# Router and final norm by columns, and the recurrence products between the first projections, in a four-layer fp32 kernel

## What is computed

```python
def rmsnorm(x, g):
    y = xf * lax.rsqrt(jnp.mean(xf * xf, axis=-1, keepdims=True) + EPS)
    return (y * g.astype(jnp.float32)).astype(x.dtype)

# first mixer, HGRN2 part (chunks of 64 tokens, 4 heads of 128)
    scores = jnp.einsum('bhnck,bhnsk->bhncs', q_dec, kh * jnp.exp(-bcum))   # then the causal mask
    o_intra = jnp.einsum('bhncs,bhnsv->bhncv', scores, vh)
    chunk_upd = jnp.einsum('bhnck,bhncv->bhnkv', kh * jnp.exp(b_last - bcum), vh)
    _, S_prev = lax.scan(step, S0, ...)                                     # S = dec * S + upd
    o = o_intra + jnp.einsum('bhnck,bhnkv->bhncv', q_dec, S_prev)           # then a norm per head
```

## Time and profile before

| | us |
|---|---|
| median of three timed runs (2555.94 to 2558.72) | 2557.13 |
| the profiled execution's own time | 2546.73 |
| its span, from the first to the last instruction | 2545.0 |
| the 24 tiles of `even_in` on PE | 25.6 to 110.5 |
| the rest of the first mixer, up to the last tile of `mixT` | 110.5 to 158.9 |
| first tile of `even_out` taken by ACT | 163.5 |
| last S5 output products | 1403.4 to 1409.6 |
| `s5_glu` | 1409.6 to 1466.2 |
| router, up to the first expert product | 1466.2 to 1500.7 |
| experts, up to the last `down` product | 1500.7 to 2519.1 |
| last spread, final norm, output | 2519.1 to 2545.0 |

### The profile page before, as it was taken

One profiled execution on the slowest core, in us unless ns is written; L12 is line 12 of the kernel. 1 busy time (PEld: TensorE's weight loads), 2 busy tenths in 40 slices (PEclk: granted clock), 3 DMA queues, 4 the chain that ended last, 5 costly groups with the idle time before them and its releaser, 6 DMA issues.

```text
span 2545.0 us, 62471 instructions
## 1 busy us (share of the span) xinstructions
PE 2320.7 (91%) x28556; PEld 2047.2 (80%) x28556; DVE 657.6 (26%) x1469; ACT 475.4 (19%) x1019; POOL 75.0 (3%) x31
## 2 busy tenths in 40 slices
PE   7989999998999899999765979999999999999997
PEld 6767887757888767888532778899999889999997
DVE  1334323133322343112699120111110111111102
ACT  2312122122221243001322111111111111111111
POOL 0000000000000000000253000000000000000000
PEclk9979999999999999999877989999999999999999
DMA  7312344232243142344200068989998989998993
GB/s 287 116 54 96 149 155 159 83 116 100 100 155 159 54 166 100 122 159 165 99 0 33 1 277 330 349 339 360 348 360 337 349 328 357 344 355 329 374 347 118
DMA packets 42271, 523.46 MB, mean 206 GB/s; under 512 B 4785, under 2 KB 4914, under 8 KB 5810
## 3 DMA queue, kind: packets, MB, share of 16 engines
q1 hardware_dynamic: 42034, 519.74, 53.0%
HBM read 518.68 MB, written 1.05 MB: 204 GB/s over the span
## 4 chain that ended last, share of the span: by engine, by line
PE 85%; DVE 9%; issue 3%; ACT 2%; DMA 0%; SPq 0%; DVEq 0%; ACTq 0%
PE ps L1244 24%; PE ps L820 17%; PE ps L799 12%; PE ps L1257 12%; PE ps L831 9%; PE ps L781 2%; PE ps L1002 1%; PE ps L1232 1%; DVE scr L1705 1%; PE ps L845 1%; PE ps L1203 1%; DVE rstd L1359 1%; DVE proj L1705 1%; PE ps L945 1%; PE ps L988 1%
## 5 line engine op out<-in xcount | busy, mean ns | idle before, releaser
L1244 PE MATMUL ps<-scr,slot 128*64 128x96 f32 x14336 | 651.5, 246 | 30.2 <-issue 29.2
L1244 PEld LDWEIGHTS ps<-scr,slot 128*64 128x64 f32 x14336 | 619.5, 137 | 37.8 <-issue 37.5
L820 PE MATMUL ps<-hT,slot 128*128 128x256 f32 x2016 | 445.4, 379 | 0.0
L820 PEld LDWEIGHTS ps<-hT,slot 128*128 128x128 f32 x2016 | 383.0, 190 | 52.1
L1257 PE MATMUL ps<-scr,slot 128*64 128x96 f32 x7168 | 354.9, 247 | 19.2 <-issue 19.1
L1257 PEld LDWEIGHTS ps<-scr,slot 128*64 128x64 f32 x7168 | 321.6, 137 | 36.6 <-issue 36.5
L799 PE MATMUL ps<-hT,slot 128*128 128x256 f32 x1120 | 246.5, 381 | 9.7 <-DVE hT L1346 7.6
L799 PEld LDWEIGHTS ps<-hT,slot 128*128 128x128 f32 x1120 | 211.2, 190 | 44.9 <-issue 16.9
L831 PE MATMUL ps<-scr,slot 128*128 128x256 f32 x1056 | 242.3, 383 | 4.8 <-DVE scr L1562 4.8
L831 PEld LDWEIGHTS ps<-scr,slot 128*128 128x128 f32 x1056 | 202.7, 192 | 34.6 <-DVE scr L1562 6.5
L1805 DVE TENSOR_TENSOR scr<-scr,ps 128x96 f32<-128x96 f32 x224 | 56.4, 252 | 649.0 <-PE ps L1244 649.0
(11 more groups left out here) (308 smaller groups left out, 1521.3 us busy)
## 6 DMA issues: line engine op xcount, KB each, us to landing
slot<-in_w_moe SPq DMA_DIRECT2D x224, 1536.0 KB, 8.7
slot<-in_w_ffn SPq DMA_DIRECT2D x33, 3072.0 KB, 10.2
slot<-in_w_even_in SPq DMA_DIRECT2D x4, 3072.0 KB, 22.9
slot<-in_w_odd_qk SPq DMA_DIRECT2D x2, 3072.0 KB, 9.9
slot<-in_w_s_glu SPq DMA_DIRECT2D x2, 3072.0 KB, 10.6
slot<-in_w_odd_v SPq DMA_DIRECT2D x2, 2048.0 KB, 7.9
slot<-in_w_even_out SPq DMA_DIRECT2D x1, 3072.0 KB, 9.9
slot<-in_w_odd_out SPq DMA_DIRECT2D x1, 3072.0 KB, 10.2
```

Of the source, the lines that this page charges most:

```text
L820: m = pe.matmul(pair(f, k), w[:, o:o + P], hT[:, c], start=c == 0, stop=c == KD - 1, skip_group_check=True)
L1244: m = pe.matmul(pair(f, k)[s:s + STRIP, 0:CAP], w[:, o:o + STRIP], xg[e % 2][:, c], start=c == 0, stop=c == KD - 1, skip_group_check=True)
```

## The change

**First mixer.** The weight columns are laid out in another order (0 to 3 forget, 4 to 7 values, 8 to 11 RG-LRU branch, 12 to 15 q, 16 to 19 output gates, 20 to 23 RG-LRU gate), the ring of the projection shrinks to two PSUM banks, and PE puts each group of recurrence products between two projection tiles. ACT and DVE are ordered to match. The last multiplication of the RG-LRU, one of 1024 columns, becomes four of 256 at the end of DVE's chain. No product is added or taken away here.

**S5.** The 16 output products of a group are ordered so that neighbours go to different column groups.

**Router.** DVE multiplies `xT` by the norm weights as each tile is made, inside the loop over `s5_glu`. PE then makes, for each of the 8 tiles, logits from these, the sum of squares with the squares as the stationary side and one column of ones, and the transposes. The root of the mean square is a number per token (per partition) now, and is applied where it matters: to the difference of the two logits and, as a factor, in `pick`. The branch on PE tests for 0 and has the gathered form first, the dense one behind it.

**End.** The last expert spreads over three PSUM banks, and releases `xT` tile by tile. The final norm goes by columns as the router does, the root is applied in the copies, and these are shared by ACT and DVE.

```diff
             def hgrn_rglru():                                  # PE
-                pe.wait_ge(tile_taken, 12)
...
+                for i in range(tiles):
+                    project(i)
+                    if i == 8:
+                        turn_values()
+                    if i == 9:
+                        turn_keys()
+                    if i == 11:
+                        updates()
+                        gate_products(0)
+                        gate_products(1)
+                    if i == 12:
+                        gate_products(2)
+                        gate_products(3)
+                    if i == 16:
+                        scores()
+                    if i in (18, 19):
+                        outputs(i - 18)
+                    if i in (20, 21):
+                        head_sums(i - 20)
...
             def outputs(q):                                    # PE, S5
-                    for j in range(4):
-                        k = 32 * j
-                        terms = [(r, x[q % 2]) for r, x in ((0, sA), (0, sC), (1, sB), (1, sD))]
-                        for i, (r, x) in enumerate(terms):
+                    terms = [(r, x[q % 2]) for r, x in ((0, sA), (0, sC), (1, sB), (1, sD))]
+                    for i, (r, x) in enumerate(terms):
+                        for j in range(4):
+                            k = 32 * j
...
             def router():                                      # PE
-                total("m3")
...
+                for c in range(KD):
+                    pe.wait_ge(h_ready, H0["m3"] + c + 1)
+                    for g in range(2):
+                        pe.matmul(ps[:, 2, g * 8:g * 8 + 8], yT[:, c, g * P:(g + 1) * P],
+                                  wr[:, c, :], start=c == g == 0, stop=c == KD - 1,
+                                  skip_group_check=True)
+                    pe.wait_ge(sq_ready, SQ0["m3"] + c + 1)
+                    for g in range(2):
+                        m = pe.matmul(ps[:, 2, 16 + g:17 + g], sq[:, c, g * P:(g + 1) * P],
+                                      ones[:, 0:1], start=False, stop=c == KD - 1,
+                                      skip_group_check=True)
...
+                        m = pe.transpose(turned_chunk(g, c), yT[:, c, g * P:(g + 1) * P], ident)
...
-                with pe.If(pe.value_load(crowded[0:1, 0:1], min_val=0, max_val=1) == 1):
+                with pe.If(pe.value_load(crowded[0:1, 0:1], min_val=0, max_val=1) == 0):
+                    experts_gathered()
+                with pe.Else():
                     experts_dense()
-                with pe.Else():
-                    experts_gathered()
...
+            def final_norm():                                  # ACT
+                act.activation(stat[:, 0, 0:1], ones[:, 0:1], ACT.Sqrt)
+                for c in range(KD):
+                    act.wait_ge(x_ready, (X_VERSION["mf"] - 1) * KD + c + 1)
+                    act.activation(sq[:, c], xT[:, c], ACT.Square).then_inc(sq_ready, 1)
+                    act.activation(hT[:, c], xT[:, c], ACT.Copy, scale=v("final_norm", c)
+                                   ).then_inc(h_ready, 1)
...
             def router():                                      # DVE
-                pre_norm("m3", xT, hT, "ffn_norm", 8)
...
+                    dve.tensor_scalar(pick[:, g], count, posm[:, g, e:e + 1], col[:, 2 + g:3 + g],
+                                      ALU.is_equal, ALU.mult).then_inc(mo["pick"], 1)
```

More of the change, by code:

```diff
@@ L273, in build_program @@
         rt = {n: sem("rt_" + n) for n in (
-            "logits", "diff", "exp", "comb", "spread", "taken")}
+            "logits", "sums", "root", "diff", "exp", "comb", "spread", "taken", "diag", "hturned")}
+        fin = {n: sem("fin_" + n) for n in ("sums", "root", "rstd")}
+        out_taken_act, out_taken_dve = sem("out_taken_act"), sem("out_taken_dve")
         moe_loaded = [sem(f"moe_loaded{i}") for i in range(HALVES)]
@@ L482, in hgrn_rglru @@
                                ).then_inc(hg["logf"], 1)
-                for i in range(16, 20):
-                    take("even_in", i, xbp[:, i - 16, 3:3 + T])
+                take("even_in", 5, proj[:, 9])
+                take("even_in", 6, proj[:, 10])
                 act.wait_ge(hg["bcum"], 4)
@@ L718, in router @@
             def router():
-                pre_norm("m3")
+                squares("m3", xT, x_ready, (X_VERSION["m3"] - 1) * KD)
+                for n in range(4):
+                    act.wait_ge(mo["hturned"], n // 2 + 1)
+                    g, half = n % 2, n // 2
+                    act.activation(vtok[:, g, half * 512:half * 512 + 512], ps[:, g, :], ACT.Copy
+                                   ).then_inc(mo["htaken"], 1)
+                act.wait_ge(rt["sums"], 1)
+                act.activation(col[:, 0:2], col[:, 24:26], ACT.Sqrt, bias=EPS, scale=1.0 / D
+                               ).then_inc(rt["root"], 1)
                 act.wait_ge(rt["diff"], 2)
```

458 lines of the change are left out of this document (276 added, 182 removed).

## The result

The changed kernel takes **2527.22 us** (median of 4 runs, 2522.43 to 2531.44), the kernel before in the same session 2556.53 (4 runs, 2549.56 to 2558.72): ratio **0.9875, 95% interval 0.9851 to 0.9899**, 1.2% faster. The forecast was 2521.5 with a range of 2505 to 2536. The execution profiled took 2525.31 us, its span is 2523.6 and its mean granted clock 0.964.

A forecast was written before the change was run, and what follows sets the result against it. PE was taken as the bound, with gains only where it idles or runs at half clock: first mixer 23.5, S5 2.0, router 8.1, end 2.0, together 35.6 us; 2557.1 - 35.6 = 2521.5, range 2505 to 2536.

The forecast's parts named there:

- the sum: Whole kernel: gains of 23.5 (first mixer), 2.0 (S5), 8.1 (router) and 2.0 (end) make 35.6 us.
- First mixer, 23.5 forecast: First mixer: products move between projection tiles, first `even_out` tile ends at 140.0 instead of 163.5; gain between 11 and 28.
- five more products end its first tile: Start of `even_out`: three products done when DVE's heads end at 137.8, five more end the first tile at 140.0.
- the second step that failed: First mixer: 56 output records, 0.31 us each at half clock, take half of that at full clock, 8.7 us.
- Rival (b): First mixer: outputs of 64 columns let the clock fall inside the projections; gain 11 to 15, time 2532; chance 0.16.
- S5, 2.0 forecast: Last group of S5 outputs: 32 records take 4.3 us instead of 6.25 by overlapping; gain between 0 and 3.
- Router, 8.1 forecast: Router to experts: PE falls through into the gathered form, first expert product at 1492.5 instead of 1500.65; gain 4 to 12.
- End, gain of 2.0 forecast: End: far branch taken at 3 us, two norm tiles at full clock, six at half; from gain 8 to loss 4.5.
- Rival (c): End and router: no stall at the end and full clock in both column-wise norms; time 2512; chance 0.08.
- (a): End: the far branch costs as much as at the router, losing 4.5 instead of gaining 2; time 2528; chance 0.18.
- (d): Experts: new code position brings 100 more late code fetches, 79 us; time 2600, slower by 43; chance 0.03.
- (e): First mixer: the change fails, for instance ACT's order holds up the ring of two; no gain, 2545; chance 0.05.

The follow-up runs named there:

- the later session: The kernel before and the changed kernel, unaltered, timed again beside a version with four further edits: medians 2556.88 and 2525.5 us, ratio 0.9897.
- the root and the pieces: Changed kernel plus four edits: early root of two heads, mixer outputs in eight pieces, woven router tiles, final norm in both branch arms; 2513.5 us, ratio 0.9846.
- the pieces: Changed kernel with the first mixer's outputs in eight pieces between products of tiles 19 and 20, not two blocks; 2526.41 us, one run, mixer 118.43.
- the arm: Changed kernel with PE's final norm written into both arms of its branch; 2515.9 us, ratio to before 0.9854, end 19.70 us.

## Why the prediction was right or wrong

**The time.** 2527.2 lies in the range and 5.7 above the forecast. On medians the change is worth 29 us (31 in the later session), and that is what the 35.6 of the sum is to be compared with. On the two profiled executions it is 21.4, and taken from them the forecast would have been 2511.1, 14 too low. The difference lies in the profile of before: at 2546.73 it is below all timed runs of its session and within 0.5 us of the fastest of the 11 later ones, 10.4 below the median, while after's is only 1.9 below its own. The sum had no term for that (4.2 us of it stand in the experts and 0.4 in the start, and after's end was 2.4 slower than that of six executions on average), and adding the 10.4 back put it right. Term by term the sum was too large by 7.75 us at the mixer and, against the average of six ends, 0.7 at the end, and too small by 1.35 up to the last S5 output: 7.1, where the medians show 35.6 - 29.3 = 6.3.

**First mixer, 23.5 forecast, 15.75 measured.** The mechanism was right: no recurrence product behind the last projection, PE waiting in `even_out` for `mixT`, DVE's chain last. The size was off by 7.75, and the profile splits it. Up to ACT's taking of tile 21 the stream was 5.9 us longer than worked out (104.97 from its start instead of 99.1): 3.0 in the first unit at half clock, 1.4 because an output takes 0.18 us and not the 0.155 I took as half of the earlier trace rows, 0.3 for the updates (2.91 instead of 2.6), 1.2 for tile 20, which took 4.74 behind the outputs. ACT's and DVE's parts (2.4 and 10.7 us) came out within 0.2 us. The last 1.9 is `even_out` at PEclk 0.64 behind PE's pause; the step "five more products end its first tile" priced them at full clock. So 6.1 of the 7.8 us are the clock (3.0, 1.2 and 1.9), and the step that failed by size is the sum's assumption of PEclk 1.00 from the first record to the last. In other executions the three parts are shared out differently, but the total is the same within 1.6. Where the clock did stay up, the forecast holds: with the root and the pieces the whole stretch ran at 1.00 and took 113.49, against 137.9 - 23.5 = 114.4 (columns as above).

```profile
25.19:138.68 113.49, 112.19 (x565) 94.63 (x566) 46.81 (x76) 43.93 (x68) 1.80 (x1) 1.00 0.31 123
```

That isn't the forecast's kernel, since the root stands ahead of tile 21 in it; that more than makes up for outputs priced too low. This pricing, of an output at half its half-clock time, is the second step that failed, by 1.4 us. I had excluded a fixed time near 0.31 by the scores of the earlier trace rows, 0.064 us a record; but they have weights of 64 columns, the outputs of 128, and full clock took the outputs only to 0.18. Whether the width of the weights makes the difference no run tried. Rival (b) named the fall of the clock, with a gain of 11 to 15, and the pieces confirm it. In size, too, after lies nearer to it than to the forecast.

**S5, 2.0 forecast, 2.8 measured** on the last group. The upper bound of 3 was nearly reached: four records overlap, where the earlier trace rows showed three. The old order gives it back.

**Router, 8.1 forecast, 8.0 measured.** Term by term as well: tiles at 1.1 and 2.2 were 1.07 and 2.02, four and four, the fall came 4.5 us behind the last dense record (4.4 assumed), the first expert product followed 5.64 us behind the pick's start (5.5). The fetch was a conclusion from one row and is now shown: cutting the code that is jumped over removed 6.2 us in the kernel before, and the packet of instructions lies in the stall. Of the gain of 8.0 the inversion made 5.9; with the dense form first again the rest of the router's change gave 2.2 up to the pick (26.78 against 28.99). By the Trainium skill, "Runtime: NRT & Kernel Launch", section "Instruction fetch mechanics", a branch breaks the sequential prefetch; the runs agree, with 5.9 us at the router and 2.65 to 3.13 us of idle time at the end.

**End, gain of 2.0 forecast, loss of 1.1 measured.** The fetch was taken at 3 us between bounds of 1.5 and 8; PE was idle for 3.13. What was off stands around it: in this execution the first spreads ran at a reduced clock (0.9 us each instead of 0.47), and the clock was at 0.50 from the first sum, not after two tiles. In five more executions of the same end the first sum came 9.5 to 9.9 us behind the last `down` instead of 11.67, and the end took 22.8 to 25.2, a gain of 0.7 to 3.1 on before's 25.93. The forecast is right for those. But it did not see the size of the opportunity: the inversion did not pay (5.9 for 7.0 on average), and the rivals that I gave compared ends with a fetch, never the same change without the inversion. Rival (c) asked for no stall and full clock in both norms; the arm gave that at the end alone, and 2515.9 where (c) said 2512.

**Other rivals.** (a) is false: idle for 3.1, not 6 us. That the median, 2527.2, lies next to its 2528 is chance: the 6 us are missing at the mixer instead. (d), more gaps in the experts: 4.2 us more in one pair of executions, 43 were asked for. (e) is false: no wait of L936 for ACT is in the profile.

## What to carry to other kernels

A branch of PE that jumps over long code cost 6 us here beside a full weight stream and 3 us with the DMA idle, and in the second place the work behind it ran at a low clock as well: invert it only if what follows the branch goes into the arm, and look at both ends before counting the gain. Short TensorE records (64 columns, 8, 1) were worth putting between 256-column records, a few at a time: in two blocks of 5 us they slowed themselves and the dense tile behind them. A pause of PE that a data chain forces can cost more than its length, by the clock behind it, so shortening the chain by 3.4 us gave 5.6. And before a sum is made against one profiled execution, look where that execution lies among the timed runs: a sum of stretches is to be taken off the median.

## What the hardware showed that I had not expected

- PEclk fell during busy stretches: PE had no idle time in 119 to 125 (3.00 of 3.00 us), made records of 64 columns up to 121.9 and of 256 behind them, and the clock was 0.81 and then 0.62.
- Records of 64 columns with weights of 128 columns take 0.18 us at full clock, hardly less than the 0.22 of 256 columns.
- The same code from the same point ran its first 96 records in 20.96 to 24.0 us, by the clock at which it happened to start; and the end of equal code took 22.8 to 27.0 us, for the most part for the same reason.
- Four products in four column groups ran four at a time, 0.108 us a record at half clock against 0.21 at the same clock in the old order.
- A taken branch of PE shows in the trace as one long instruction (6.84 us over some 700 products, 0.21 over the short form, 0.08 where it falls through), with a 16 KB packet of the instruction queue in it, and PE went on 1.42 to 1.52 us behind the packet's end in all eight long jumps ahead of work.
